# Weight halves interleaved in SBUF, moving tiles read and PSUM banks written from the last column to the first

## The chip, the core and the metric

The kernel runs on one core of a Trainium2 chip. Its engines are TensorE (PE, with its weight loads shown apart as PEld), VectorE (DVE), ScalarE (ACT), GpSimd (POOL) and SyncE (SP, which here only issues transfers). The metric is the device time of one execution in microseconds (us), lower is better; the median of three runs before the change is 2625.01 us.

## What is computed

The reference runs two transformer stacks of two layers one after the other on a sequence of 512 tokens and a width of 1024, all in float32. Cut to what matters:

```python
# first_block
x += even_mixer(rmsnorm(x), ...)      # gated linear recurrence + retention, 4 heads each
x += swiglu(rmsnorm(x), w_gate_up, w_down)   # hidden 2816
x += odd_mixer(rmsnorm(x), ...)       # compressed / selected / windowed attention, 16 heads
x += swiglu(rmsnorm(x), ...)
# second_block: per layer shift, scale and gate from c @ ada_w
x = layer_norm(ALPHA * x + g1 * mixer(modulate(x)))       # differential + grouped attention, then a conv mixer
x = layer_norm(ALPHA * x + g2 * (square(relu(h @ w1)) @ w2))   # hidden 4096
```

Most of the arithmetic is `h @ w`: a 512x1024 activation times weight matrices that are read once. It has to come out close to full float32 precision.

## The kernel before

**Products in three parts.** The activations are kept feature-major, as tiles of 128 partitions x 8 blocks x 512 tokens. TensorE multiplies float32r operands here (a rounded float32). So each operand is split in two: `h_hi` is `h` rounded to float32r and `h_lo` the rest, and the same for the weights (`w_hi`, `w_lo`). A product of one 128x128 weight block with one 128x512 block of tokens is three matmuls into the same PSUM bank: `w_hi*hi`, `w_hi*lo`, `w_lo*hi`. Each has its own weight load of 128 columns.

**Units.** The weights of the whole program are cut into 384 units of 128x1024 (8 blocks of 128x128). `PLAN` lists the stages (mix_in, out0, ffn0_up0, ...), and a unit's 8 blocks x 3 parts are 24 matmuls, one output bank. Units run in pairs: slot 0 and slot 1. `unit` (L2425) does the ordinary ones, `mix_unit` (L2566) those of the first stage, L2687 the first two of out0, and `half_steps` (L2469) those at nine stage ends and beginnings, in two halves of 256 tokens. These last also use slots 2 and 3 (`more_w_hi2`, ...).

**How a unit's weights arrive.** SyncE loads a unit into `w_raw[s]`. ScalarE copies it, rounded, to `w_hi[s]` (L679; L685 for the further slots) once the matmuls of the unit that used the slot before are done (`unit_done`). VectorE subtracts: `w_lo[s] = w_raw[s] - w_hi[s]` (L1403, L1409). TensorE waits for `w_lo_done` and for its bank to be free (`bank_free`). The orders of all engines are written out by hand, as loops over pairs; no scheduler decides anything.

**Where the tiles lie.** Each tile has a fixed byte address in its partition. `sb` hands out addresses one after the other, in multiples of 64. In the compiled program `x`, `h_hi`, `h_lo`, `g_hi` and `g_lo` begin at 16512, 32896, 49280, 65664 and 82048, all 128 more than a multiple of 512. A block of tokens is 2048 bytes and a weight block 512 bytes, so every block in them also begins at 128 modulo 512. The same holds for `w_hi` and `w_lo` of slots 0 and 1 (106624, 110720, 114816, 118912). `w_hi` and `w_lo` of slots 2 and 3 begin at 210880 and every 4096 bytes after it, which is 448 modulo 512. A weight load reads 128 consecutive elements, a matmul 512 (or 256) consecutive ones, and it writes its bank from the first column to the last.

Of the kernel before, what the change touches and what calls it, by code (L numbers as in the profile page):

```python
# [19 lines left out]
F32R = mybir.dt.float32r  # L20
# [5 lines left out]
P = 128  # L26
T = 512
TT = T // P
D = 1024
KT = D // P  # L30
# [106 lines left out]
def mix_bank(u):  # L137

    return u if u < 2 else u + 4 if u < 4 else u % 2
# [32 lines left out]
def program(nc, dram, out):  # L172
    with ExitStack() as ctx:
# [3 lines left out]
        cursor = [nc.sbuf_base]  # L177
        cursor[0] = (cursor[0] + 63) // 64 * 64

        def size_of(shape):  # L180
            n = 4
            for k in shape[1:]:
                n *= k
            return (n + 63) // 64 * 64

        def sb(name, shape, dt=F32):
            t = nc.alloc_sbuf_tensor_at(name, shape, dt, offset=cursor[0])
            cursor[0] += size_of(shape)
            return t
# [12 lines left out]
        H_AT = cursor[0]  # L202
# [3 lines left out]
        G_LO_AT = cursor[0]  # L206
        g_lo = sb("g_lo", [P, KT, T], F32R)
        w_raw = [sb(f"w_raw{s}", [P, KT, P]) for s in range(2)]
        w_hi = [sb(f"w_hi{s}", [P, KT, P], F32R) for s in range(2)]
        w_lo = [sb(f"w_lo{s}", [P, KT, P], F32R) for s in range(2)]  # L210
        ada_raw = sb("ada_raw", [P, D])
        ada_col = sb("ada_col", [P, 1])
        tab = sb("tab", [P, NTAB])
# [7 lines left out]
        psum = [banks[:, b, :] for b in range(8)]  # L221
# [17 lines left out]
        def place(prefix, at, items):  # L239

            made = {}
            for name, shape, dt in items:
                made[name] = nc.alloc_sbuf_tensor_at(prefix + name, shape, dt, offset=at)
                at += size_of(shape)
            return made, at
# [28 lines left out]
        ROW_SCALE_AT = (LIMIT - 4 * T) // 64 * 64  # L274
# [13 lines left out]
        def turned_probs(i):  # L288

            return (S3, S)[i // 2 % 2]["pt"][:, i % 2]  # L290
# [9 lines left out]
        def slope_table(h):  # L300
            return S["raw"][:, h, :] if h < 2 else S3["bias"][:, h % 4, :]

        c_row = place("rows_", ARENA + 28 * 4 * T, [("c", [P, 2, D], F32)])[0]["c"]
        W4, _ = place("more_", ROW_SCALE_AT - 4 * 4 * D, [(f"w_{part}{s}", [P, KT, P], F32R) for s in (2, 3)
                                                          for part in ("hi", "lo")])
        w_hi += [W4["w_hi2"], W4["w_hi3"]]
        w_lo += [W4["w_lo2"], W4["w_lo3"]]
        keep = [("aq", [P, 4, T]), ("bq", [P, 4, T]), ("ak", [P, 4, NK]), ("bk", [P, 2, NK]),
                ("av", [P, KEY_TILES, T]), ("bv", [P, KEY_TILES, P]), ("ao", [P, 4, T]), ("lam", [P, 4]),
                ("nm", [P, 2, 2]), ("sum", [P, 2, 2]), ("r", [P, 2, 2])]  # L310
        B2 = overlay("attn_", keep)
        ATT_HIGH = sum(size_of(shape) for _, shape in keep)
        B3 = overlay("attn1_", [("ctx", [P, KT, CTX]), ("avt", [P, 4, NK]), ("bvt", [P, NK]), ("bkt", [P, NK]),
                                ("rope", [P, 2, T]), ("sq", [P, NK]), ("rstd", [P, NK])], ATT_HIGH)
# [101 lines left out]
        def half_cols(half):  # L416
            return slice(T // 2 * half, T // 2 * half + T // 2)
# [1991 lines left out]
        def _(pe):  # L2409
            def unit(i, s, moving, kts=KT, fresh=None, inside=None):  # L2410

                pe.wait_ge(w_lo_done, 2 * i + s + 1)
                if not isinstance(i, int) or i > 0:
                    pe.wait_ge(bank_free[s], i)
                for bank, hi, lo in moving:
                    for n, k in enumerate(fresh[2][:kts] if fresh else range(kts)):
                        if fresh:  # L2420
                            pe.wait_ge(fresh[0], fresh[1] + n + 1)
                        if inside and n == inside[0]:
                            inside[1]()
                        for a, (w, m) in enumerate(((w_hi, hi), (w_hi, lo), (w_lo, hi))):
                            mm = pe.matmul(bank, w[s][:, k, :], m[:, k, :], start=(n == 0 and a == 0),  # L2425
                                           stop=(n == kts - 1 and a == 2))
                mm.then_inc(unit_done, 1)

# [26 lines left out]
            def square_means(r):  # L2455
                pe.wait_ge(s2_done, r + 1)
                token_sums(N["s2"], 0).then_inc(stat_done, 1)

            def spread_scales(r):
                pe.wait_ge(diag_done, r + 1)  # L2460
                pe.matmul(psum[2], ones, N["diag"][:].rearrange("p t n -> p (t n)"), start=True, stop=True)\
                    .then_inc(scale_done, 1)

            def half_steps(bank, slot, half, hi, lo, steps, kts=KT):

                cols = half_cols(half)
                for k in steps:
                    for a, (w, m) in enumerate(((w_hi, hi), (w_hi, lo), (w_lo, hi))):
                        mm = pe.matmul(bank[:, cols], w[slot][:, k, :], m[:, k, cols], start=(k == 0 and a == 0),  # L2469
                                       stop=(k == kts - 1 and a == 2))  # L2470
                return mm

# [77 lines left out]
            def mix_unit(u):  # L2550

                s, bank = u % 2, psum[mix_bank(u)]
                pe.wait_ge(w_lo_done, u + 1)
                if u > 3:
                    pe.wait_ge(bank_free[s], u // 2)
                for k in range(KT):
                    if u == 0:
                        pe.wait_ge(h_ready, k + 1)
                    if u == 2 and k == 2:
                        square_means(0)  # L2560
                    if u == 2 and k == 6:
                        spread_scales(0)
                    if u == MIX_UNITS - 1 and k == 5:
                        stat(7)
                    for a, (w, m) in enumerate(((w_hi, h_hi), (w_hi, h_lo), (w_lo, h_hi))):
                        mm = pe.matmul(bank, w[s][:, k, :], m[:, k, :], start=(k == 0 and a == 0),  # L2566
                                       stop=(k == KT - 1 and a == 2))
                mm.then_inc(unit_done, 1)

# [54 lines left out]
            def stat(n):  # L2624

                pe.wait_ge(o_sq, 2 * n + 2)
                pe.matmul(psum[2 + n % 4], ones, head(n)[1], start=True, stop=True).then_inc(o_stat, 1)
# [53 lines left out]
            for k, s in [(k, s) for part in (range(4), range(4, KT - 1), (KT - 1,)) for s in range(2) for k in part]:  # L2681
                if k == 0:
                    pe.wait_ge(w_lo_done, 2 * p0 + s + 1)
                    pe.wait_ge(bank_free[s], p0)
                pe.wait_ge(g_ready, k + 1)
                for a, (w, m) in enumerate(((w_hi, g_hi), (w_hi, g_lo), (w_lo, g_hi))):
                    mm = pe.matmul(psum[s], w[s][:, k, :], m[:, k, :], start=(k == 0 and a == 0),  # L2687
                                   stop=(k == KT - 1 and a == 2))
                if k == KT - 1:
                    mm.then_inc(unit_done, 1)  # L2690
# [124 lines left out]
            for j in range(NSA_JOBS + 5):  # L2815
# [8 lines left out]
                if j < NSA_JOBS:  # L2824
                    m, qi, half = j // 8, (j // 2) % TT, j % 2
# [4 lines left out]
                    if qi < 2:  # L2830
                        both_keys = banks[:, 4 - 2 * (j % 2), 0:2 * W].rearrange("p (b n) -> p b n", b=2)
                        for part in range(2):
                            mm = pe.matmul(both_keys, q, S["ks"][:, :, part, m // 4, 0:W], start=(part == 0),
                                           stop=(part == 1))
                    else:
                        for b in range(2):
                            for part in range(2):
                                mm = pe.matmul(banks[:, 4 - 2 * (j % 2) + b, 0:W], q, S["ks"][:, b, part, m // 4, 0:W],  # L2838
                                               start=(part == 0), stop=(part == 1))
                    mm.then_inc(n_s, 1)  # L2840
                if 3 <= j < NSA_JOBS + 3:
                    i = j - 3
                    qi = (i // 2) % TT
                    for b in range(2):
# [7 lines left out]
                        for t in range(qi + 1):  # L2852
                            mm = pe.transpose(psum[6 + b][:, t * P:(t + 1) * P], S3["e"][:, i % 3, b, t * P:(t + 1) * P],  # L2853
                                              ident)
                        mm.then_inc(n_t, 1)
                if j >= 5:
                    i, b = (j - 5) // 2 * 2, (j - 5) % 2
                    m, qi = i // 8, (i // 2) % TT
# [14 lines left out]
                    for t in range(qi + 1):  # L2873
                        for half in range(2):
                            last = b == 1 and t == qi
                            mm = pe.matmul(o[half], S["v"][:, b, t, g, :],  # L2876
                                           turned_probs(i + half)[:, b, t * P:(t + 1) * P], start=False, stop=last)
# [107 lines left out]
            for j in range(ATT_JOBS + 2):  # L2985
# [6 lines left out]
                if j < ATT_JOBS:  # L2992
                    qi = j % 4
                    m = j // 4 if j < 16 else (j - 16) // 4
                    for b in range(2):
# [5 lines left out]
                        for a, (c0, c1) in enumerate(((0, T), (T, NK))):  # L3001
                            mm = pe.matmul(banks[:, 2 + 2 * b + a, 0:c1 - c0], q, keys[:, c0:c1], start=True, stop=True)  # L3002
# [161 lines left out]
```

## Time and profile before

| | before |
|---|---|
| runs | 2629.20, 2623.85, 2625.01 us; median 2625.01 |
| span of the profiled execution | 2627.9 us |
| TensorE busy | 97%, 13070 matmuls |
| VectorE, ScalarE, GpSimd busy | 60%, 40%, 10% |
| granted TensorE clock, mean | 0.990 |
| HBM | 274 MB read, 106 GB/s |

The profile is of one execution, taken by the hardware profiler; its span is from the first to the last instruction, and no other time of that execution is given. Its span lies 2.9 us above the median of the runs. Matmuls overlap in the records: their durations are modelled with their way through the array, so a row says 390 ns where the next matmul starts 227 ns later. What a matmul costs in a stream is the distance from start to start, or a stretch of the chain of waits divided by its count, and not the mean of its group. Shapes are given as partitions x elements; an element step is not shown in them.

### The profile page before, as it was taken

The numbers are of one execution on the slowest core, as the hardware profiler recorded it, in microseconds if no ns is written. First come the engines' busy times: TensorE is split into PE (matmuls) and PEld (weight loads), VectorE is DVE, ScalarE is ACT, GpSimd is POOL, SyncE is SP. The second block draws the span as 40 slices with busy tenths as digits, with TensorE's granted clock in tenths as the row PEclk, the third lists the DMA queues.
The fourth block names the chain that finished last, engine by engine and source line by source line (L and its number), as shares of the span: only waits on it lengthen the run. The fifth ranks groups of instructions, "written<-read, shape, count | busy, mean of one in ns | idle before, by whom it ended". The sixth has DMA issues, their size and how long they took to land.

```text
span 2627.9 us, 37789 instructions
## 1 busy us (share of the span) xinstructions
PE 2557.7 (97%) x13070; PEld 2102.4 (80%) x13070; DVE 1581.3 (60%) x2460; ACT 1048.3 (40%) x1663; POOL 258.4 (10%) x187
## 2 busy tenths in 40 slices
PE   8999999999999999999989999999999999999997
PEld 6887788888877778888878776788888888888886
DVE  6764665656578866565665786655555665644445
ACT  5334522223347852222353266553223522522333
POOL 2320100000320010000030100310000301300002
PEclk9999999999999999999999999999999999999999
DMA  3221344444320034444432100234444243332222
GB/s 133 73 88 65 118 137 144 144 145 151 135 73 25 26 113 144 144 144 144 144 121 73 41 1 1 81 112 144 144 149 140 96 144 116 104 100 96 96 96 80
DMA packets 79337, 277.46 MB, mean 106 GB/s; under 512 B 8448, under 2 KB 11904, under 8 KB 78720
## 3 DMA queue, kind: packets, MB, share of 16 engines
q1 hardware_dynamic: 58560, 205.55, 23.6%
q10 hardware_dynamic: 20672, 70.51, 8.1%
q8 instruction: 67, 1.10, 0.2%
q14 instruction: 38, 0.31, 0.0%
HBM read 273.92 MB, written 2.10 MB: 105 GB/s over the span
## 4 chain that ended last, share of the span: by engine, by line
PE 85%; DVE 8%; ACT 3%; issue 2%; DMA 1%; POOL 1%; ACTq 0%; DVEq 0%; SPq 0%; POOLq 0%
PE banks L2425 64%; PE banks L2566 5%; PE banks L3002 2%; PE banks L2469 2%; DVE w_lo L1403 1%; PE banks L2944 1%; PE banks L2600 1%; PE banks L2876 1%; DMA w_raw<-weights 1%; PE banks L2853 1%; PE banks L2956 1%; ACT w_hi L679 1%; PE banks L2973 1%; DVE nsa_e L1968 1%; PE banks L2838 1%
## 5 line engine op out<-in xcount | busy, mean ns | idle before, releaser
L679 ACT ACTIVATE w_hi<-w_raw 128x1024 fp32r<-128x1024 f32 x367 | 386.4, 1053 | 621.5 <-PE banks L2425 514.9
L2425 PE MATMUL banks<-h_hi,w_hi 128*128 128x512 f32 x1600 | 628.2, 393 | 1.1 <-DVE w_lo L1403 0.7
L2425 PE MATMUL banks<-h_hi,w_lo 128*128 128x512 f32 x1600 | 623.4, 390 | 0.0
L2425 PE MATMUL banks<-h_lo,w_hi 128*128 128x512 f32 x1600 | 623.2, 389 | 0.0
L1403 DVE TENSOR_TENSOR w_lo<-w_raw,w_hi 128x1024 fp32r<-128x1024 f32 x367 | 474.2, 1292 | 108.7 <-ACT w_hi L679 92.1
L2425 PE MATMUL banks<-g_hi,w_hi 128*128 128x512 f32 (+1 forms) x1108 | 427.7, 386 | 9.8 <-DVE w_lo L1403 8.8
L2425 PE MATMUL banks<-g_lo,w_hi 128*128 128x512 f32 (+1 forms) x1108 | 423.9, 383 | 0.0
L2425 PE MATMUL banks<-g_hi,w_lo 128*128 128x512 f32 (+1 forms) x1108 | 423.7, 382 | 0.0
L2425 PEld LDWEIGHTS banks<-h_hi,w_hi 128*128 128x128 f32 x1600 | 300.5, 188 | 66.5 <-issue 2.8
L2425 PEld LDWEIGHTS banks<-h_lo,w_hi 128*128 128x128 f32 x1600 | 300.6, 188 | 62.8 <-issue 1.7
L2425 PEld LDWEIGHTS banks<-h_hi,w_lo 128*128 128x128 f32 x1600 | 300.4, 188 | 62.9
L2425 PEld LDWEIGHTS banks<-g_hi,w_hi 128*128 128x128 f32 x1108 | 208.7, 188 | 58.6 <-DVE w_lo L1403 14.8
L2425 PEld LDWEIGHTS banks<-g_lo,w_hi 128*128 128x128 f32 x1108 | 208.8, 188 | 40.7 <-issue 1.0
L2425 PEld LDWEIGHTS banks<-g_hi,w_lo 128*128 128x128 f32 x1108 | 208.8, 188 | 40.5
L2030 DVE SCALAR_TENSOR_TENSOR x<-banks,mod,x 128x512 f32 (+1 forms) x72 | 54.0, 749 | 163.4 <-PE banks L2425 163.2
L1426 DVE CUSTOM_DVE_ANT_0 ada_raw<-ada_raw,rows_c 128x1024 f32<-128x1024 f32 x112 | 138.7, 1238 | 0.0
L2338 DVE TENSOR_TENSOR ffn_hid<-ffn_act 128x512 f32<-128x512 f32 x64 | 44.3, 693 | 131.8 <-ACT ffn_act L1347 131.8
L2566 PE MATMUL banks<-h_hi,w_hi 128*128 128x512 f32 x256 | 104.5, 408 | 10.1 <-DVE w_lo L1403 10.1
L1347 ACT ACTIVATE ffn_act<-banks 128x512 f32<-128x512 f32 x64 | 38.3, 598 | 189.1 <-PE banks L2425 184.3
L523 POOL TENSOR_TENSOR norm_s<-norm_xc 128x512 f32<-128x512 f32 x4 | 8.8, 2200 | 952.5 <-DVE norm_xc L2035 952.5
L2566 PE MATMUL banks<-h_hi,w_lo 128*128 128x512 f32 x256 | 101.3, 396 | 0.0
L2566 PE MATMUL banks<-h_lo,w_hi 128*128 128x512 f32 x256 | 101.0, 395 | 0.0
(411 smaller groups left out, 3290.8 us busy)
## 6 DMA issues: line engine op xcount, KB each, us to landing
w_raw<-weights SPq DMA_DIRECT2D x384, 512.0 KB, 3.3
ada_raw<-ada ACTq DMA_DIRECT2D x112, 512.0 KB, 3.3
nsa_bias<-nsa_bias ACTq DMA_DIRECT2D x6, 512.0 KB, 3.4
x<-x SPq DMA_DIRECT2D x4, 512.0 KB, 6.6
out<-x SPq DMA_DIRECT2D x8, 256.0 KB, 2.1
mix_cum<-ret_tab ACTq DMA_DIRECT2D x1, 1024.0 KB, 4.7
rows_c<-c_rows ACTq DMA_DIRECT2D x1, 1024.0 KB, 5.6
nsa_w<-cmp_w ACTq DMA_DIRECT2D x1, 1024.0 KB, 5.4
```

The source lines that it names most:

```text
L679: act.activation(w_hi[s][:], w_raw[s][:], ACT.Copy).then_inc(w_hi_done, 1)
L1347: act.activation(F["act"][:, s, :], psum[s], ACT.Relu).then_inc(bank_free[s], 1)
L1403: dve.tensor_tensor(w_lo[s][:], w_raw[s][:], w_hi[s][:].bitcast(F32), ALU.subtract)\
L1426: dve.tensor_tensor_reduce(ada_raw[:], ada_raw[:], c_row[:, who, :], 1.0, 0.0, ALU.mult, ALU.add, ada_col[:]).then_inc(ada_done, 1)
L1968: dve.tensor_tensor_reduce(S3["e"][:, j % 3, b, 0:W], scores, slope_table(h)[:, T - W:T], -1.0, 3.0e38, ALU.add, ALU.min, S["nm"][:, j % 2 ...
L2030: dve.scalar_tensor_tensor(xm, row(psum[s]), mod[:, bass.ds(8 * part + m, 1), 0], xm, ALU.mult, ALU.add).then_inc(bank_free[s], 1)
L2338: dve.tensor_tensor(F["hid"][:, s, :], F["act"][:, s, :], F["act"][:, s, :], ALU.mult)\
L2425: mm = pe.matmul(bank, w[s][:, k, :], m[:, k, :], start=(n == 0 and a == 0), stop=(n == kts - 1 and a == 2))
L2469: mm = pe.matmul(bank[:, cols], w[slot][:, k, :], m[:, k, cols], start=(k == 0 and a == 0), stop=(k == kts - 1 and a == 2))
L2566: mm = pe.matmul(bank, w[s][:, k, :], m[:, k, :], start=(k == 0 and a == 0), stop=(k == KT - 1 and a == 2))
L2600: mm = pe.matmul(grams[:, cols(t)], left[:, h, cols(t)], right[:, h, cols(t)], start=True, stop=True)
L3002: mm = pe.matmul(banks[:, 2 + 2 * b + a, 0:c1 - c0], q, keys[:, c0:c1], start=True, stop=True)
```

## The change

It consists of three edits and changes no instruction's place: each engine issues the same instructions in the same order before and after, with other addresses and steps.

1. `w_hi[s]` and `w_lo[s]` become the even and the odd elements of one tile `w_split[s]` of 128 x 8 x 128 x 2. ScalarE writes, VectorE reads and writes, and the weight loads read with a step of two elements, 8 bytes.
2. The four tiles get set addresses modulo 512: slot 0 at 128, slot 1 at 192, slot 3 at 160, slot 2 at 256. (Compared with the 128 of the moving tiles these are 0, 64, 32 and 128 bytes further.) The tiles allocated after them lie 512 bytes higher than before.
3. All matmuls that read these weights read their moving tile from its last column to its first and write the bank in the same order. What stands in the bank is the same.

```diff
         w_raw = [sb(f"w_raw{s}", [P, KT, P]) for s in range(2)]
-        w_hi = [sb(f"w_hi{s}", [P, KT, P], F32R) for s in range(2)]
-        w_lo = [sb(f"w_lo{s}", [P, KT, P], F32R) for s in range(2)]
+        w_split = []
+        for s, start in enumerate((128, 192)):
+            cursor[0] += (start - cursor[0]) % 512
+            w_split.append(sb(f"w_split{s}", [P, KT, P, 2], F32R))
+        cursor[0] += (H_AT - cursor[0]) % 512
...
-        W4, _ = place("more_", ROW_SCALE_AT - 4 * 4 * D, [(f"w_{part}{s}", [P, KT, P], F32R) for s in (2, 3)
-                                                          for part in ("hi", "lo")])
-        w_hi += [W4["w_hi2"], W4["w_hi3"]]
-        w_lo += [W4["w_lo2"], W4["w_lo3"]]
+        more_at = ROW_SCALE_AT
+        for s, start in ((3, 160), (2, 256)):
+            more_at -= 2 * 4 * D
+            more_at -= (more_at - start) % 512
+            w_split.insert(2, place("more_", more_at, [(f"w_split{s}", [P, KT, P, 2], F32R)])[0][f"w_split{s}"])
+        w_hi, w_lo = ([pair[:, :, :, part] for pair in w_split] for part in range(2))
...
-                            mm = pe.matmul(bank, w[s][:, k, :], m[:, k, :], start=(n == 0 and a == 0),
+                            mm = pe.matmul(bank[:, ::-1], w[s][:, k, :], m[:, k, ::-1], start=(n == 0 and a == 0),
                                            stop=(n == kts - 1 and a == 2))
```

The last edit is made in the same way in `half_steps`, `mix_unit` and at L2687. The gate product at L2714 (24 matmuls of 512 columns, weights in tiles of their own) and all plain float32 matmuls stay as they are.

## Rows read from the trace of the kernel before

**Rows 1.** The page: span, busy time by engine, granted clock.

```profile
span 2627.9 us, 37789 instructions
PE 2557.7 (97%) x13070; PEld 2102.4 (80%) x13070; DVE 1581.3 (60%) x2460; ACT 1048.3 (40%) x1663; POOL 258.4 (10%) x187
PEclk9999999999999999999999999999999999999999
```

**Rows 2.** The page: the chain that ended last, by line.

```profile
PE banks L2425 64%; PE banks L2566 5%; PE banks L3002 2%; PE banks L2469 2%; DVE w_lo L1403 1%; PE banks L2944 1%; PE banks L2600 1%; PE banks L2876 1%; DMA w_raw<-weights 1%; PE banks L2853 1%; PE banks L2956 1%; ACT w_hi L679 1%; PE banks L2973 1%; DVE nsa_e L1968 1%; PE banks L2838 1%
```

**Rows 3.** TensorE's groups by shape: busy us, mean ns, idle before.

```profile
L2425 PE MATMUL banks<-h_hi,w_hi 128*128 128x512 f32 x1600 | 628.2, 393 | 1.1 <-DVE w_lo L1403 0.7 <-DVE attn_aq L2203 0.2
...
L2425 PE MATMUL banks<-g_hi,w_hi 128*128 128x512 f32 x1028 | 405.1, 394 | 9.8 <-DVE w_lo L1403 8.8 <-DVE g_lo L2319 0.9 <-DVE g_lo L2273 0.2
...
L2566 PE MATMUL banks<-h_hi,w_hi 128*128 128x512 f32 x256 | 104.5, 408 | 10.1 <-DVE w_lo L1403 10.1
...
L2425 PE MATMUL banks<-g_hi,w_hi 128*128 128x256 f32 x80 | 22.6, 283 | 0.0
L2469 PE MATMUL banks<-g_hi,more_w_hi 128*128 128x256 f32 x76 | 22.4, 294 | 0.0
L2469 PE MATMUL banks<-g_hi,w_hi 128*128 128x256 f32 x76 | 21.9, 288 | 0.0
L2469 PE MATMUL banks<-h_hi,w_hi 128*128 128x256 f32 x64 | 21.7, 339 | 3.6 <-POOL h_lo L538 3.6
...
L2469 PE MATMUL banks<-h_hi,more_w_hi 128*128 128x256 f32 x64 | 19.9, 311 | 0.0
...
L2687 PE MATMUL banks<-g_hi,w_hi 128*128 128x512 f32 x16 | 6.6, 412 | 1.3 <-DVE g_lo L1574 1.3
```

**Rows 4.** The chain in order of time: start us, us, what, count.

```profile
67.71 3.81 PE banks L2600 x32
...
83.38 3.57 PE banks L2600 x32
...
189.50 3.46 PE banks L2608 x16
...
335.64 314.49 PE banks L2425 x1386
...
2270.74 300.84 PE banks L2425 x1326
```

**Rows 5.** Matmuls in order of time at the last stage: start us, us, what.

```profile
2598.80 0.28 PE L2469 MATMUL banks<-g_hi,w_hi 128*128 128x256 f32 x1
...
2601.67 0.28 PE L2469 MATMUL banks<-g_hi,more_w_hi 128*128 128x256 f32 x1
...
2604.49 0.28 PE L2469 MATMUL banks<-g_hi,w_hi 128*128 128x256 f32 x1
```

**Rows 6.** The same view at 1335 us, slot 2.

```profile
1335.31 0.28 PE L2469 MATMUL banks<-g_lo,more_w_hi 128*128 128x256 f32 x1
...
1337.13 0.28 PE L2469 MATMUL banks<-g_hi,more_w_lo 128*128 128x256 f32 x1
```

**Rows 7.** Lines L1684, L1403 and L679: duration ns min/median/max, first and last start.

```profile
L1684 DVE TENSOR_TENSOR mix_d<-mix_d,mix_k x9: 1207/1212/1221, 61.1 to 181.1; 128x1024 f32<-128x1024 f32 x9
...
L1403 DVE TENSOR_TENSOR w_lo<-w_raw,w_hi x367: 1212/1226/2414, 7.6 to 2594.5; 128x1024 fp32r<-128x1024 f32 x184
...
L679 ACT ACTIVATE w_hi<-w_raw x367: 1038/1050/1067, 6.6 to 2593.0; 128x1024 fp32r<-128x1024 f32 x184
```

**Rows 8.** Waits: who waited for whom, us in total, times, longest.

```profile
ACT w_hi L679 <- PE banks L2425: 514.9, 132, 9.8
```

**Rows 9.** Busy us of each engine in one stretch of ordinary units; clock, DMA share, GB/s.

```profile
1000.00:1300.00 300.00, 300.00 (x1326) 248.56 (x1324) 169.04 (x232) 78.85 (x94) 0.00 (x0) 1.00 0.44 145
```

**Rows 10.** The page: the weight transfer, KB each, us to landing.

```profile
w_raw<-weights SPq DMA_DIRECT2D x384, 512.0 KB, 3.3
```

More of the change, by code:

```diff
@@ L2468, in half_steps @@
                     for a, (w, m) in enumerate(((w_hi, hi), (w_hi, lo), (w_lo, hi))):
-                        mm = pe.matmul(bank[:, cols], w[slot][:, k, :], m[:, k, cols], start=(k == 0 and a == 0),
+                        mm = pe.matmul(bank[:, cols][:, ::-1], w[slot][:, k, :], m[:, k, cols][:, ::-1], start=(k == 0 and a == 0),
                                        stop=(k == kts - 1 and a == 2))
@@ L2565, in mix_unit @@
                     for a, (w, m) in enumerate(((w_hi, h_hi), (w_hi, h_lo), (w_lo, h_hi))):
-                        mm = pe.matmul(bank, w[s][:, k, :], m[:, k, :], start=(k == 0 and a == 0),
+                        mm = pe.matmul(bank[:, ::-1], w[s][:, k, :], m[:, k, ::-1], start=(k == 0 and a == 0),
                                        stop=(k == KT - 1 and a == 2))
@@ L2686, in _ @@
                 for a, (w, m) in enumerate(((w_hi, g_hi), (w_hi, g_lo), (w_lo, g_hi))):
-                    mm = pe.matmul(psum[s], w[s][:, k, :], m[:, k, :], start=(k == 0 and a == 0),
+                    mm = pe.matmul(psum[s][:, ::-1], w[s][:, k, :], m[:, k, ::-1], start=(k == 0 and a == 0),
                                    stop=(k == KT - 1 and a == 2))
```

## The prediction

> **What bounds the kernel now.** I read the page's busy times first: TensorE is busy 97% of 2627.9 us, VectorE 60%, ScalarE 40% [rows 1]. Busy alone would not do, since matmul records overlap, so the chain of waits came next: 64% of the span is TensorE at L2425, 5% at L2566, 2% at L2469, and the weight preparation (L1403, L679) stands there with 1% each [rows 2]. These are the matmuls that the change touches. The groups by shape give their number [rows 3]: of 512 columns there are 3 parts each of 1600 and 1028 at L2425, 256 at L2566 and 16 at L2687, so 3 x 2900 = 8700. Of 256 columns there are 3 x 80 at L2425, 3 x (76 + 64) at L2469 from slots 0 and 1, so 660, and 3 x (76 + 64) = 420 from slots 2 and 3. The idle time before the L2425 groups is 1.1 and 9.8 us: in ordinary stages TensorE waits for nobody. Its pace there decides.
>
> The chain in order of time gives that pace. 1386 matmuls follow each other in 314.49 us and 1326 in 300.84 us: 226.9 ns each, in both stretches [rows 4]. The clock granted there is 1.00, the upper of the two levels, 2.4 GHz [rows 9], at which 512 columns take 512/2.4 = 213.3 ns. So each matmul costs 13.6 ns more than its columns. Over 8700 of them that is 118 us, and it is all that this change can reach, since it removes no instruction and moves none.
>
> **Is that rest a fixed price?** Three readings say that it is not wholly one.
> - L2608 is plain float32 with 256 columns and takes 3.46/16 = 216.2 ns [rows 4]. That is 512 steps of the same clock plus 2.9 ns, with a weight load per matmul as well. The array can run through 213.3 ns with a load beside it and lose 3 ns instead of 13.6. The difference to the float32r matmuls is that those fetch a moving column at every step.
> - The same 256-column matmul has another pace with another weight tile. From slot 0 (weights at 128 modulo 512, like the moving tile) 24 of them take 2601.67 - 2598.80 = 2.87 us, 119.6 ns each; from slot 2 (at 448) 24 take 2604.49 - 2601.67 = 2.82 us, 117.5 ns each [rows 5]. Over the 106.7 ns of 256 columns this is 12.9 and 10.8 ns.
> - The same slot 2, started after a pause of TensorE, takes (1337.13 - 1335.31)/16 = 113.8 ns, 7.1 over its columns [rows 6]. Only the two streams' position in time differs.
>
> So the rest depends on where the weight load reads and on when it does so relative to the moving tile. I read it as the two reads meeting in SBUF. It is also nearly the same at 512 and at 256 columns (13.6 and 12.9 ns): it belongs to the load and not to the column count. The Trainium skill, in "TensorE: Matmul & The Clock Gate", section "Step-by-step: what each phase is for", says otherwise: two independent SBUF read ports, and loading the next weights takes nothing from the running matmul. By that rule the 13.6 ns would be a fixed price and the change worth nothing; the trace does not agree, because of the 119.6 against 113.8 ns just read.
>
> **The change part by part.**
> - *Steps and direction.* Before, a load walks 512 bytes in its time and the moving read walks faster, so they pass each other. A load of 128 columns takes at most 3.57/32 = 111.6 ns, the pace of L2600, where it is beside a matmul of 128 columns [rows 4]; in 107 to 112 ns the moving read walks about 1024 bytes. With a step of 8 bytes the load walks 1024 bytes as well. If both walk the same way they keep their distance; that holds for a moving tile read backwards if the chip takes the weights from the last column to the first. The addresses modulo 512 then set the distance. Bounds: from nothing left but the 2.9 ns of L2608, so 226.9 - 216.2 = 10.7 ns less, to a meeting that is worse than before (the rivals). I take 9.4 ns less, a pace of 217.5 ns, since 10.7 is what a stream with only half the fetches shows and four distances will hardly all be perfect. 8700 x 9.4 = 81.8 us. The 256-column ones can fall to the load's own 111.6 ns at best, 8.0 x 660 + 5.9 x 420 = 7.8 us; half of the L2469 ones wait for other engines anyway, so I take 4 us. Sum 86 us.
> - *The strided copy and subtraction.* L1684 at its first start (61.1 us) works on elements 8 bytes apart in both inputs and the output, and later on runs of 2 to 64 elements; its nine durations lie between 1207 and 1221 ns, w_lo's median is 1226 [rows 7]. So VectorE pays nothing for the step. For ScalarE's write no row is that near: from 0 to twice its 1050 ns. I take 0, since it handles an element per step as VectorE does. What hides it in ordinary units: it waits 514.9 us for matmuls before it starts [rows 8], and copy and subtraction together are 2.3 us of a unit's 24 x 226.9 = 5.4 us. Without cover, at stage changes, doubling it would double its 1% of the chain, +26 us.
> - *A faster TensorE and the others.* A unit would take 5.2 us. Transfer, copy and subtraction (3.3 + 1.1 + 1.2 = 5.6 us, [rows 7, 10]) are spread over the two units between the uses of a slot, 10.4 us. VectorE is busy 169 of 300 us in such a stretch, the DMA engines 44% [rows 9], so 4% more pace starves nobody. For the few exposed waits that stay what they are I add 1 us.
> - *Writing a bank backwards.* No matmul in this trace writes or reads with a step other than 1. From below: 0, as the columns are the same and contiguous. From above: half pace, 2 x 216.2 = 432 ns for 512 columns, which L2608's 256 at 216.2 scale to. I take 0, the direction of a contiguous run being the smaller step from what is there.
> - *Addresses of the later tiles, +512 bytes:* 0, modulo 512 they are unchanged.
>
> The profiled span would become 2627.9 - 86 + 1 = 2543 us. It stands 2.9 us above the runs' median, so 2540 us.
>
> **The rivals.**
> 1. *Part of it.* The distance suits one slot of the two that do the ordinary units, or the meetings are halved: 8700 x 4.7 = 41 us + 2 us, 2582 us. For it: slot 2 against slot 0 moved only 2.1 ns at steady running [rows 5], so places differ, but little. Against: there the streams still passed each other.
> 2. *Nothing.* The 13.6 ns are mostly the price of swapping weights under float32r, and the readings above show only its variable edge; or the compiled program reads in its own order whatever is asked. 2625 us. For it: nearly one value, 226.9 ns, over 2700 matmuls. Against: rows 5 and 6.
> 3. *Slower, opposed walks.* If the chip takes weights from the first column to the last, the reversed moving read now runs against them: 2048 bytes of passing per load in place of 512 (same way) or, if the extra was measured on opposed walks, 1536. With the extra in proportion to the passing, 13.6 x 2048/1536 = 18.1 ns, +4.5 ns x 8700 = 39 us: 2664 us. It decides from the point where a load's meetings number more than before. The same sign has the case that slot 0, whose weights lie at the moving tile's own 128 modulo 512, walks on top of it: if that costs the load's whole 111.6 ns beside 213.3, half of the 8700 pay 98 ns each, +426 us; anything between is possible. For it: nothing in the trace tells the order of a weight load. Against: equal places gave 119.6 ns before, no disaster, though on passing walks.
> 4. *A step or a backward run costs its engine half its pace.* The load: 2 x 111.6 = 223 ns stays under the present 226.9, but not under 119.6: +104 ns x 1080 = 112 us for the 256-column ones, about 2710 us with nothing gained elsewhere. The bank: (432 - 226.9) ns x 8700 = 1784 us, 4410 us.
>
> In "PSUM — Partial Sum Buffer", section "Specifications (TRN2)", the Trainium skill says that PSUM has lines of 8 bytes and any access that is not contiguous slows matmuls significantly; if a step of -1 counts as such, rival 4's second price applies, and no run here shows that yet.
>
> **How the numbers follow.** The forecast (most of the rest goes) 0.52; rival 1 0.16; rival 2 0.08; rival 3 0.17; rival 4 0.07, of which 0.02 for the bank. The forecast's own range is 2522 (all 10.7 ns at 8700, 93 us, + 8 us, and 2 us of spread) to 2562 us. With rival 1 and 2 it holds 0.76; to leave out no more than 2 in 10 the range goes on to rival 3's nearer price: 2522 to 2666 us. What a measurement of this kernel can tell from no change is 0.2%, 5 us. Faster: 0.52 + 0.16 - 0.01 = 0.67. Same: 0.08 + 0.01 for the smallest partial gains = 0.09. Slower: 0.17 + 0.07 = 0.24.
>
> **What would show it.** In the chain after the change, the long L2425 stretches divided by their counts: 217.5 ns as forecast, about 222 for rival 1 (then probably two paces, alternating by slot every 24 matmuls), 226.9 for rival 2, 231 or more for rival 3. L2714, whose weights are not interleaved, should stay at 227 ns. The 256-column runs should go to 112 to 114 ns, and show over 200 if the load halves. The rows of L1403 and L679 should keep 1226 and 1050 ns at the median. The forecast is wrong if the pace of any slot rises, or if the pace falls and TensorE's idle time before L2425 grows from 11 us to tens.

## The result: 2681.44 us, 2.1% slower

The change takes 2681.44 us (median of 4 runs, 2679.66 to 2689.09) against 2627.11 us before (now also 4 runs, 2623.85 to 2633.36): the ratio is 1.0208, with a 95% interval of [1.0188, 1.0229]. I had forecast 2540 us, a gain, with a range up to 2666 us. It lost 54 us.

The page after, with the lines that answer to [rows 1, 2]:

```profile
span 2687.3 us, 37789 instructions
...
PE 2621.3 (98%) x13070; PEld 2172.3 (81%) x13070; DVE 1578.2 (59%) x2460; ACT 1096.1 (41%) x1663; POOL 257.8 (10%) x187
...
PEclk9999999999999999999999999999999999999999
...
PE banks L2430 65%; PE banks L2571 6%; PE banks L3007 2%; PE banks L2474 2%; PE banks L2949 1%; DVE w_split L1408 1%; DMA w_raw<-weights 1%; PE banks L2605 1%; PE banks L2881 1%; PE banks L2858 1%; ACT w_split L684 1%; PE banks L2961 1%; PE banks L2978 1%; DVE nsa_e L1973 1%; PE banks L2843 1%
```

Line numbers are 5 higher than before. The instructions are as many as before and the path has the same members. No new wait appears: the chain is again TensorE's own stream. The chain in order of time (start us, us, what, count) shows where the time went; these rows answer to [rows 4]:

```profile
338.63 323.69 PE banks L2430 x1386
...
711.75 5.46 PE banks L2719 x24
...
1013.65 321.73 PE banks L2430 x1368
...
2320.72 309.65 PE banks L2430 x1326
```

The same 1386 and 1326 matmuls took 314.49 and 300.84 us before. So each takes 233.5 ns in place of 226.9, 6.6 ns more, and 8700 x 6.6 = 57 us. That accounts for the loss. L2719, the gate product whose weights and direction did not change, kept its 227 ns (5.46/24).

One long stretch is slower still: the 1368 matmuls from 1013.65 us take 235.2 ns each. The starts of the single matmuls in the trace split it by slot. Between 1015 and 1330 us a matmul of slot 0, whose weights lie at the moving tile's own place, takes 236.7 ns and one of slot 1 takes 233.3 ns; in the stretches at 338 and 1755 us both slots take 233.3 ns. That is 1368 x (235.2 - 233.5) = 2.3 us in all, and what puts a stretch into one state or the other stays open.

The clock granted in this slower stretch is 1.00 as before, so it is not the clock (columns: stretch; us; busy us of PE, PEld, DVE, ACT and POOL; clock; DMA share; GB/s), which answers to [rows 9]:

```profile
1020.00:1320.00 300.00, 300.00 (x1278) 249.14 (x1278) 162.75 (x223) 83.24 (x92) 0.00 (x0) 1.00 0.42 140
```

The matmuls of 256 columns kept their pace. In the last stage 24 of them from slot 2 take 2663.91 - 2661.08 = 2.83 us, 117.9 ns each, where [rows 5] had 117.5:

```profile
2661.08 0.28 PE L2474 MATMUL banks<-g_hi,more_w_split 128*128 128x256 f32 x1
...
2663.91 0.28 PE L2474 MATMUL banks<-g_hi,w_split 128*128 128x256 f32 x1
```

The copy and the subtraction (duration ns min/median/max) answer to [rows 7]: the subtraction is unchanged at 1227 ns, ScalarE's strided write costs 1181 instead of 1050 ns.

```profile
L684 ACT ACTIVATE w_split<-w_raw x367: 1133/1181/1211, 6.5 to 2652.5; 128x1024 fp32r<-128x1024 f32 x184
```
```profile
L1408 DVE TENSOR_TENSOR w_split<-w_raw,w_split x367: 1214/1227/2419, 7.7 to 2653.8; 128x1024 fp32r<-128x1024 f32 x184
```

### The profile page after: what moved, and what is told of

It is laid out like the page before. It is cut to its first block, busy times and chain, and to the rows that moved or that the text cites. A ratio compares the mean times of both kernels' runs of the same rounds, so it can differ in the third digit from the quotient of the medians.

```text
span 2687.3 us, 37789 instructions
## 1 busy us (share of the span) xinstructions
PE 2621.3 (98%) x13070; PEld 2172.3 (81%) x13070; DVE 1578.2 (59%) x2460; ACT 1096.1 (41%) x1663; POOL 257.8 (10%) x187
## 4 chain that ended last, share of the span: by engine, by line
PE 86%; DVE 7%; ACT 3%; issue 1%; DMA 1%; POOL 0%; ACTq 0%; DVEq 0%; SPq 0%
PE banks L2430 65%; PE banks L2571 6%; PE banks L3007 2%; PE banks L2474 2%; PE banks L2949 1%; DVE w_split L1408 1%; DMA w_raw<-weights 1%; PE banks L2605 1%; PE banks L2881 1%; PE banks L2858 1%; ACT w_split L684 1%; PE banks L2961 1%; PE banks L2978 1%; DVE nsa_e L1973 1%; PE banks L2843 1%
## 5 line engine op out<-in xcount | busy, mean ns | idle before, releaser
L2430 PE MATMUL banks<-h_hi,w_split 128*128 128x512 f32 x3200 | 1022.1, 399 | 0.8 <-DVE w_split L1408 0.4
L2430 PEld LDWEIGHTS banks<-h_hi,w_split 128*128 128x128 f32 x3200 | 624.6, 195 | 126.5 <-issue 2.7
L2430 PE MATMUL banks<-g_hi,w_split 128*128 128x512 f32 (+1 forms) x2216 | 688.5, 391 | 9.4 <-DVE w_split L1408 8.0
L684 ACT ACTIVATE w_split<-w_raw 128x1024 fp32r<-128x1024 f32 x367 | 432.6, 1179 | 630.6 <-PE banks L2430 522.0
L2430 PE MATMUL banks<-h_lo,w_split 128*128 128x512 f32 x1600 | 635.9, 397 | 0.0
L1408 DVE TENSOR_TENSOR w_split<-w_raw,w_split 128x1024 fp32r<-128x1024 f32 x367 | 472.8, 1288 | 146.7 <-ACT w_split L684 142.0
L2430 PEld LDWEIGHTS banks<-g_hi,w_split 128*128 128x128 f32 x2216 | 427.2, 195 | 96.7 <-DVE w_split L1408 13.9
L2430 PE MATMUL banks<-g_lo,w_split 128*128 128x512 f32 (+1 forms) x1108 | 431.1, 389 | 0.0
L2430 PEld LDWEIGHTS banks<-h_lo,w_split 128*128 128x128 f32 x1600 | 312.3, 195 | 62.2 <-issue 1.6
L2430 PEld LDWEIGHTS banks<-g_lo,w_split 128*128 128x128 f32 x1108 | 216.4, 195 | 39.9 <-issue 0.9
L2571 PE MATMUL banks<-h_hi,w_split 128*128 128x512 f32 x512 | 170.5, 407 | 9.6 <-DVE w_split L1408 9.6
L2571 PEld LDWEIGHTS banks<-h_hi,w_split 128*128 128x128 f32 x512 | 101.1, 197 | 29.8 <-issue 9.7
L2571 PE MATMUL banks<-h_lo,w_split 128*128 128x512 f32 x256 | 102.5, 400 | 0.0
```

The source lines that it names most:

```text
L684: act.activation(w_hi[s][:], w_raw[s][:], ACT.Copy).then_inc(w_hi_done, 1)
L1408: dve.tensor_tensor(w_lo[s][:], w_raw[s][:], w_hi[s][:].bitcast(F32), ALU.subtract)\
L2430: mm = pe.matmul(bank[:, ::-1], w[s][:, k, :], m[:, k, ::-1], start=(n == 0 and a == 0), stop=(n == kts - 1 and a == 2))
L2571: mm = pe.matmul(bank[:, ::-1], w[s][:, k, :], m[:, k, ::-1], start=(k == 0 and a == 0), stop=(k == KT - 1 and a == 2))
```

## The experiments

Two kinds were run: the full kernel with parts of the change, and small kernels with nothing but streams of matmuls, one source line for each stream, whose pace is a row of the chain divided by its count. Ratios are to the kernel before, on the same chip, with 95% intervals.

### The two parts of the change apart

Interleaving alone (`i1_interleave`):

```diff
-  mm = pe.matmul(bank[:, ::-1], w[s][:, k, :], m[:, k, ::-1], ...
+  mm = pe.matmul(bank, w[s][:, k, :], m[:, k, :], ...        # on the changed kernel, all four places
```

> The change without its backward part: weight halves interleaved at the changed addresses, moving tiles and banks first to last. After the change the L2430 streams run at 233.3 ns per matmul against 226.9 before, in both slots. Theory STEP (a weight load that walks with 8 bytes meets the moving read more often or for longer, whichever way that one goes): 233 ns again, some 2680 us. Theory BACKWARD (reading or writing backward costs): 227 ns, 2627 us. Theory OPPOSED (the two reads walk against each other after the change): turned round they walk together, the pace falls below 226.9 ns, 2530 to 2600 us. In all of them the ScalarE copy keeps its 1179 ns mean of the changed kernel, since its write is still strided.

Backward alone (`i2_backward`), the other way round on the kernel before:

```diff
-  mm = pe.matmul(bank, w[s][:, k, :], m[:, k, :], ...
+  mm = pe.matmul(bank[:, ::-1], w[s][:, k, :], m[:, k, ::-1], ...        # on the kernel before, all four places
```

> The backward part alone: weight halves in separate contiguous tiles at their old addresses, moving tiles and banks last to first. STEP: 226.9 ns, 2627 us. BACKWARD: 233 ns, some 2680 us. OPPOSED: a load of 512 bytes now walks the other way relative to the moving tile than before; the pace changes either way by a few ns. The ScalarE copy goes back to 1053 ns.

Interleaving alone: 2666.98 us, ratio 1.0137 [1.0120, 1.0154]. Backward alone: 2675.95 us, ratio 1.0177 [1.0160, 1.0194]. The same stretch of the chain, first of `i1_interleave`, then of `i2_backward`:

```profile
1741.58 307.55 PE banks L2430 x1326
```
```profile
1742.98 309.64 PE banks L2425 x1326
```

That is 231.9 and 233.5 ns. Either part alone costs 5 to 6.6 ns, and both together cost hardly more than the second one. None of the three theories fits: STEP wanted 226.9 ns from the second, BACKWARD 226.9 from the first, and OPPOSED wanted the first below 226.9.

### A map of places, steps and directions

```python
for n in range(REPEAT):     # m1_map: REPEAT 64; one such line for each (offset, step, moving, bank, columns)
    mm = pe.matmul(*operands(n, 8, 1, 1, 1, 512, 3), start=(n == 0), stop=(n == REPEAT - 1))
```

> No transformer: 81 streams of 64 float32r matmuls, 128x128 weights each with its own load, moving tile at 128 modulo 512 as in the kernel, one source line per stream, other engines idle. It computes nothing of the reference and writes x out. Four forms (weights contiguous or with an 8-byte step, moving tile and bank both forward or both backward) at 16 places of the weight tile, 32 bytes apart; a factorial of weight step, moving direction and bank direction at one place; a few with 256 columns and with a 16-byte step. Theory PLACE: the pace depends on the distance modulo 512 of the two tiles, the changed kernel's distances 0 and 64 are bad ones, and at some distance the interleaved backward form falls to 216 to 220 ns. Theory STEP: the 8-byte forms show 233 ns at every place. Theory BACKWARD: in the factorial the backward moving read or the backward bank alone shows +6 ns. The contiguous forward form at distance 0 should show 226.9 ns if the kernel's pace comes from these two reads alone, and about 216 to 220 if it comes from VectorE and ScalarE working beside it.

The chain of `m1_map`. L66, L70, L78 and L82 are contiguous and forward, with the weight tile 0, 64, 192 and 256 bytes beyond the moving tile's place modulo 512:

```profile
47.78 14.52 PE banks L66 x64
...
77.22 14.93 PE banks L70 x64
...
136.95 14.67 PE banks L78 x64
...
166.54 14.52 PE banks L82 x64
...
285.30 14.94 PE banks L98 x64
...
509.31 14.94 PE banks L128 x64
524.25 14.55 PE banks L130 x64
538.79 14.51 PE banks L132 x64
553.30 14.94 PE banks L134 x64
568.24 14.93 PE banks L136 x64
...
642.91 14.93 PE banks L146 x64
...
672.68 14.72 PE banks L150 x64
```

Three things are to be seen. First, with nothing else running, the kernel's old form still takes 14.52/64 = 226.9 ns at distance 0: the pace belongs to TensorE's own stream, VectorE and ScalarE have no part in it. Second, distance matters in that form: 226.9 ns at 0 and 256, 229 at 192, 233.3 at 64. Third, L98 to L128 are the changed form (8-byte step, backward) at 16 distances, 32 bytes apart: 233.3 ns at each of them. None of these places would have saved it, so PLACE falls for this form. The factorial at distance 0 says which direction it is: L130 all forward 227.3 ns, L132 only the bank backward 226.7, L134 only the moving tile backward 233.4, L136 both 233.3. So BACKWARD holds for the moving read and not for the bank. The interleaved form read forward costs 233.3 ns at distance 0 (L146) and 230.0 at 64 (L150), which are the distances of slots 0 and 1: STEP's 233 ns at every place is not there either. Their mean is 231.7 ns, and `i1_interleave` ran at 231.9.

### What the extra does not come from

`m2_sizes` varies one thing per stream: weight columns, tokens, banks, start flags, blocks.

```python
mm = pe.matmul(*operands(n, 0, 0, -1, 512, 1, wcols=32), ...)   # woff, moving offset, moving step, columns, bank
```

> 58 streams of 48 matmuls, otherwise as in the first map (nothing of the reference is computed). What is known: contiguous, forward, weights and moving tile at the same place modulo 256: 226.7 ns (13.4 over the columns' 213.3); every backward moving read: 233.3 ns (20.0 over) whatever the weights do; 256 columns: 120.0 at most (13.3 over). Theory WEIGHT MEETINGS (the extra is a load's read meeting the moving read): halving the weight columns to 64 halves the extra, 32 quarter it, and it does not grow with the columns from 256 to 512 in the backward form. Theory MOVING READ (the moving read itself loses a step every so many columns, backward or in a bad place more often, and the load only shifts it): the extra of the backward form grows in proportion to the columns, about 6.7 ns + 1 step of 0.42 ns per 16 columns, and stays 20 ns with 64 or 32 weight columns. Theory BANK (accumulating into the same bank is part of it): start on every matmul, or another bank for each, goes under 226 ns. Moving the moving tile and the weights together by 32 to 256 bytes should keep 226.7 if only their distance counts.

The chain of `m2_sizes`. In this order: old form; only the moving tile 64 bytes further; moving tile and weights both 64 bytes further; 256 and 320 columns forward; 256 and 320 columns backward; start on each matmul; another bank for each; one weight block and one moving block for all; 64 weight columns backward; 32 weight columns forward and backward; moving tile with an 8-byte step, forward:

```profile
30.92 10.89 PE banks L65 x48
...
164.79 11.00 PE banks L89 x48
...
208.79 10.91 PE banks L97 x48
...
272.70 5.75 PE banks L111 x48
...
284.78 7.04 PE banks L115 x48
...
341.88 5.71 PE banks L129 x48
...
347.58 7.05 PE banks L131 x48
...
418.33 10.90 PE banks L147 x48
429.23 10.88 PE banks L149 x48
...
473.09 10.88 PE banks L157 x48
...
495.01 11.20 PE banks L161 x48
...
517.32 11.11 PE banks L165 x48
528.43 11.20 PE banks L167 x48
...
550.67 21.66 PE banks L171 x48
```

BANK falls: accumulation, the bank and the block make no difference (226.7 to 227.1 ns). WEIGHT MEETINGS falls, and with it the picture behind my forecast: a backward stream that loads 32 columns of weights instead of 128 still takes 11.20/48 = 233.3 ns, and forward the small load is even worse than the large one (231.5). The weight load's position shifts the forward pace; making the load smaller never lowered it.

The first three rows show that it is the distance between the two tiles that counts. Both shifted by 64 bytes: 227.3 ns, close to no shift. The moving tile alone shifted by 64: 229.2 ns, which is what the first map gave for weights 192 bytes further, the same distance modulo 256.

MOVING READ is half right. Its 20 ns over the columns' time do stay with 64 and 32 weight columns. But they do not grow evenly with the columns: backward streams stand 12.3 ns over with 256 columns, 13.5 with 320, and 20 already with 480. Backward against forward, 256 columns take 119.0 against 119.8 ns and 320 columns 146.9 against 146.7: the backward read costs nothing there. The unchanged 117.9 ns of the changed kernel's 256-column matmuls fit this.

The last row is a warning of another size: an 8-byte step in the *moving* tile halves the pace, to 451 ns per matmul.

### The place alone, the bank alone, the best interleaved place

```diff
+  cursor[0] += 64           # i3_place: on the kernel before, weight tiles of slots 0 and 1
   w_hi = [sb(f"w_hi{s}", ...
   w_lo = [sb(f"w_lo{s}", ...
+  cursor[0] += 448          # so that all later tiles keep their place modulo 512
```

> The kernel before with one thing changed: the weight tiles of slots 0 and 1 lie 64 bytes further (192 modulo 512, so 64 beyond the moving tiles), contiguous, everything forward. The map of streams gave 233.3 ns for this distance and 226.7 for distance 0. Theory MAP (two tiles' distance modulo 256 sets the pace, in the full kernel as alone): 233.3 ns in ordinary stretches, +6.5 ns x 8700 = 57 us, about 2680 us, as slow as the whole change although nothing is interleaved or backward. If the place did not count in the kernel: 226.9 ns and 2627 us.

```diff
-  mm = pe.matmul(bank, w[s][:, k, :], m[:, k, :], ...
+  mm = pe.matmul(bank[:, ::-1], w[s][:, k, :], m[:, k, :], ...     # i4_bank
```

> The kernel before with only the banks written last column to first; the moving tiles are read forward, so every product's tokens stand in reversed order and the output is not the reference's. MAP: 226.9 ns, no change, 2627 us: the bank's direction costs nothing. If a backward bank costs by itself: up to 233 ns, 2680 us.

```diff
-  for s, start in enumerate((128, 192)):     # i5_inter64: on i1_interleave
+  for s, start in enumerate((192, 192)):
...
-  for s, start in ((3, 160), (2, 256)):
+  for s, start in ((3, 192), (2, 192)):
```

> Interleaved halves, everything forward, all four weight tiles at 192 modulo 512 (64 beyond the moving tiles), the best place for an 8-byte step in the map: 230.0 ns. The run with slot 0 at distance 0 and slot 1 at 64 showed 232.5 and 230.8 ns. MAP: 230.0 to 231 in both slots, 3.5 ns x 8700 = 30 us over before plus the strided ScalarE write: about 2658 us, some 8 us under that run, and still slower than before.

The same stretch of the chain, of `i3_place`, `i4_bank` and `i5_inter64`:

```profile
1743.29 309.64 PE banks L2427 x1326
```
```profile
1719.43 300.88 PE banks L2425 x1326
```
```profile
1729.39 305.23 PE banks L2430 x1326
```

| | map | in the kernel | ratio |
|---|---|---|---|
| weights 64 bytes further, nothing else | 233.3 ns | 233.5 ns | 1.0181 [1.0164, 1.0198] |
| bank backward, nothing else | 226.7 ns | 226.9 ns | 1.0004 [0.9994, 1.0014] |
| interleaved, forward, all at distance 64 | 230.0 ns | 230.2 ns | 1.0113 [1.0094, 1.0133] |

The map told the full kernel's pace within 0.2 ns three times. Moving the weight tiles of two slots by 64 bytes, with no other edit, costs as much as the backward part of the change.

### A grid

`m3_grid` steps the columns of a product from 128 to 512, in both directions, and adds plain float32:

```python
mm = pe.matmul(*operands(n, 0, 0, 1, 400, 3), ...)      # REPEAT 48; columns 128 to 512, step 1 and -1
mm = pe.matmul(*plain(n, 0, 0, 1, 512, 4), ...)         # the same tiles read as plain float32
```

> 60 more streams of 48 matmuls (nothing of the reference is computed), moving tile and weights at distance 0, forward and backward, with 128 to 512 columns in steps of 16 near the top, then plain float32. Theory GRID: a matmul in such a stream starts on a grid of 16 columns' time, 6.67 ns (226.7 is 34, 233.3 is 35, 120.0 is 18 of them), and direction and place only decide which one it gets: the paces at multiples of 16 columns come out as whole multiples of 6.67 ns or as mixtures of two neighbours, and 504 or 508 columns cost the same as 512. Theory PER COLUMN (a loss in proportion to the columns): the paces grow evenly with the columns. Plain float32 should show 216 ns for 256 columns as in the kernel, in either direction; if backward costs it too, the cost does not come from the rate of fetching.

The chain of `m3_grid`, all at distance 0. Forward with 400 columns (L75), 448 (L81), 508, 504 and 500 (L105 to L109); backward with 480 and 496 (L99, L101); plain float32 with 512 columns, forward and backward (L173, L175; each such product is two matmuls in the trace, so 96):

```profile
49.12 8.64 PE banks L75 x48
...
76.19 9.74 PE banks L81 x48
...
164.51 10.56 PE banks L99 x48
175.07 10.88 PE banks L101 x48
...
196.83 10.91 PE banks L105 x48
207.75 10.90 PE banks L107 x48
218.65 10.72 PE banks L109 x48
...
486.10 41.20 PE banks L173 x96
527.30 41.20 PE banks L175 x96
```

These are 180.0, 202.9, 220.0, 226.7, 227.3, 227.1 and 223.3 ns. PER COLUMN does not hold: forward, 504 and 508 columns cost what 512 do. GRID looks good at first, since 180.0, 220.0 and 226.7 ns are 27, 33 and 34 times 6.67 ns, the time of 16 columns. But of the 26 streams with a multiple of 16 columns, 256 and more, only about half have a mean near a whole number of steps, and "a mixture of two neighbours" fits any mean. The starts of the single matmuls in the trace decide it. Some streams are uniform: 400 columns forward (180 ns each), 480 backward (220), 512 forward (226 or 227) and, in the first map, 512 backward (233 or 234). Others are not on such a grid: 496 columns backward (L101) is 24 distances of 224 or 225 ns and 23 of 229, with a mean of 226.7, and 508 columns forward (L105) spread from 222 to 234 ns. So 6.67 ns is the difference between two common paces, and not a grid that matmuls start on.

Nor does the form of a stream fix its pace: 448 columns forward, with the same tiles and distance, took 9.91/48 = 206.5 ns in `m2_sizes` and 202.9 ns here. Plain float32 spends 41.20/96 = 429.2 ns on a matmul of 512 columns in either direction, about two steps of the clock per column: at half the rate of fetching the direction costs nothing.

### Is there a better place?

```python
mm = pe.matmul(*operands(n, o, 0, 1, 512, bank), ...)   # m4_fine: REPEAT 40; o = 0 to 64 elements, one stream each
mm = pe.matmul(*operands(n, o, 0, 1, 256, bank), ...)   # then 256 columns, o in steps of 4
```

> Streams of 40 matmuls (nothing of the reference is computed), contiguous and forward, the weight tile's distance in steps of 4 bytes from 0 to 256, and 256 columns in steps of 16 bytes. It looks for a distance under 226.7 ns, that is for a faster kernel than before. Theory GRID with a floor: distance 0 and 256 stay the best at 226.7 ns, all others lie between 227 and 236. If there is a place one step of 6.67 ns lower it shows 220 ns, and the kernel before with its tiles moved there would save up to 6.7 ns x 8700 = 58 us.

`m4_fine` stepped the weight tile through 65 distances of 4 bytes. No 512-column stream ran under 226.7 ns; the shortest of its rows, 9.07 us for 40, stand at distance 0 (L67 below) and at 100, 144, 156, 228 and 252 bytes. Distance 256 took 9.09, and most others lie between 230 and 237.5 ns. With 256 columns distance 64 (L205) is better than distance 0 (L197), 113.5 against 119.8 ns:

```profile
37.94 9.07 PE banks L67 x40
...
640.95 4.79 PE banks L197 x40
...
659.92 4.54 PE banks L205 x40
```

The first map has the same distance modulo 256, 320 bytes, at 7.54/64 = 117.8 ns:

```profile
1127.18 7.54 PE banks L212 x64
```

Slots 2 and 3 of the kernel before lie at exactly this distance (448 - 128 = 320). They ran at 117.5 ns in [rows 5] and at 113.8 after a pause in [rows 6]. The two maps show the same two paces, so a place can have more than one, and no run shows what chooses. Going from 117.5 to 113.5 would bring at most 420 x 4.0 = 1.7 us, less than the 5 us that can be told from no change here. Nothing in the map points to a version faster than the kernel before.

### What is left for the copy

`r1_change` is the changed kernel with no edit, and `r2_backward` is `i2_backward` again with no edit:

> The changed kernel itself once more, beside the kernel with only the backward reads, on one chip. Both pace their streams at 233.4 ns, yet the change was 1.0208 times before and the backward part alone 1.0177. Theory COPY: the rest, 0.3% or some 6 to 8 us, is ScalarE's strided write (1181 ns instead of 1049) at the stage changes, where nothing hides it: the difference stays. Theory SCATTER: it lay between chips and clock windows and goes below 2 us side by side.

> The partner of the run before: contiguous weight tiles, backward moving tiles and banks. COPY: 5 us or more under the changed kernel. SCATTER: within 2 us of it.

Side by side, in five rounds, the change stood at 1.0216 [1.0202, 1.0230] (2684.55 us) and the backward part alone at 1.0195 [1.0181, 1.0209] (2680.58 us). ScalarE's write took 1181 and 1048 ns at the median. The difference of 4 us has COPY's sign and lies between the two theories' numbers, and the intervals overlap. There is also a rival to COPY that neither theory named. First `r1_change`, then `r2_backward`:

```profile
340.33 325.99 PE banks L2430 x1386
```
```profile
339.29 323.69 PE banks L2425 x1386
```

The changed kernel again has one long stretch at 235.2 ns, this time the first one (slot 0 at 236.7 ns, slot 1 at 233.3), and that alone is 2.3 us. So what the strided write costs is some part of the 4 us, or nothing; it is not settled.

## Why the prediction was wrong

- **What bounds the kernel: right.** The stream's pace at L2425 decided, and 8700 x its change (57 us) accounts for the result. No wait came or went: TensorE's idle time before the L2430 groups is 0.8 and 9.4 us (1.1 and 9.8 before), and ScalarE still waits for the matmuls (522.0 us after, 514.9 before).
- **"The rest is not wholly a fixed price": right, but I read too much into it.** The pace does depend on place, and 64 bytes are worth 6.6 ns in the whole kernel (`i3_place`). But the 117.5 and 113.8 ns of [rows 5, 6] came from one and the same place. They are paces that a stream settles into, and not amounts of collision that a better layout takes to nothing. The sentence of the Trainium skill ("TensorE: Matmul & The Clock Gate", section "Step-by-step: what each phase is for"), that loading the next weights takes nothing from the running matmul, was weighed as the rule against the change. The runs do not bear it out for the place of the load (64 bytes cost 6.6 ns). On its amount, a smaller load never made a stream faster (32 or 128 weight columns, 233.3 ns backward).
- **"If both walk the same way they keep their distance": the step that failed.** I put the 13.6 ns down to the two reads meeting and took 9.4 of them away for equal walks. The runs show that the number of meetings does not set the cost: the backward read of 512 columns costs 233.3 ns with either weight step, at all 16 places and with a quarter of the load. In its place stands +6.6 ns for reading the moving tile backward, and +3.3 to +6.6 ns for the weights' 8-byte step read forward. What the 13.3 ns over the columns' time are at the best place stays open. Every stream here loads weights for each matmul, so the price of swapping weights (rival 2) was not tested.
- **"All that this change can reach" and the floor of 216.2 ns: wrong use of a row.** L2608 is a plain float32 stream, which fetches a column at half the rate. Its kind is insensitive to direction and place (429.2 ns both ways, and also with the weights 32 bytes further), and its 2.9 ns were not had by any float32r stream: 65 places gave 226.7 ns at the lowest.
- **The bounds of the steps.** VectorE's subtraction: 0, as read from L1684. ScalarE's write: I took 0, it is +131 ns each, and what that is worth lies within the 4 us of the last pair of runs. The 256-column matmuls: I took 4 us of gain, it is 0 (117.9 against 117.5 ns). The bank backward: 0, measured alone (1.0004). The rule of the Trainium skill ("PSUM — Partial Sum Buffer", section "Specifications (TRN2)") that an access that is not contiguous slows matmuls did not show at a step of -1.
- **The rivals.** Rival 3 had the sign, and its mark of "231 ns or more" was met, with 39 us where 57 came. Its price in proportion to the passing did not show: contiguous and interleaved weights, 1536 and 2048 bytes of passing by its count, ran backward at the same 233.3 ns. No run reversed the weight load, so whether its direction matters is open. Its second case, slot 0 at the moving tile's own place, showed faintly: 3.3 ns over slot 1, in one of the long stretches. It got 0.17 because I had made one theory of three rows and no row at all showed a backward read.

## What to carry to other kernels

When a stream of float32r matmuls runs a few per cent over its columns' time, the cause may be where its operands lie and which way they are read; a small kernel of streams, one source line each, maps this in one run of a millisecond and gave the full kernel's pace within 0.2 ns. Keep the moving tile contiguous and, with 512 columns, read forward, and put weight and moving tiles at the same place modulo 256 bytes, or measure the distance; a harmless-looking shift of 64 bytes cost 1.8% of this kernel. Read every long stretch of the trace, and each slot apart: a mean over two slots or a single stretch hides a second pace. And a floor that is read from another kind of instruction is not a floor.

## What the runs showed of the hardware that was not expected

- Float32r streams of 512 columns run at 226.7 ns or more in every form tried (213.3 ns would be the columns alone). With a backward moving read they take 233.3 ns at all 16 weight places tried; with 256 or 320 columns it costs nothing (119.0 against 119.8 ns, 146.9 against 146.7).
- The pace of a forward stream follows the distance of weight and moving tile: 226.7 ns at 0 and 256 bytes, 233.3 at 64, 229.2 at 192.
- The direction in which a bank is written costs nothing (226.7 ns forward and backward).
- An 8-byte step in the moving tile costs double (451 ns), in the weights read forward 3.3 to 6.6 ns per matmul.
- One form can have two paces: slot 2 at 117.7 and 113.3 ns, and slot 0 of the changed kernel at 233.3 and 236.7 ns, by the starts of single matmuls.
- What chooses between such paces stays open, and so does why the small weight load is worse going forward (231.5 ns with 32 columns, 226.9 with 128).
